# A hybrid layer on one core: the attention heads' tiles keep their places, and ScalarE's work within a step is put in another order

## The reference

```
z      = q k^T / sqrt(128)                     for all keys up to the query
log_1m = log_sigmoid(-z)     (0 where masked)
later  = sum of log_1m over the keys between this key and the query
w      = exp(log_sigmoid(z) + later)           (0 where masked)
out    = w v,   then out * silu(g)
```

## Time and profile before

| | |
|---|---|
| median of three executions | 2375.96 us |
| the profiled execution: time, span | 2375.72 us, 2373.8 us |
| PE busy | 2320.7 us, 98% of the span |
| DVE busy | 1498.2 us, 63% |
| POOL busy | 1262.6 us, 53% |
| ACT busy | 1060.0 us, 45% |
| granted clock of PE | 0.997 of full |

### The profile page before, as it was taken

One profiled execution on the slowest core, in us unless ns is written; L12 is line 12 of the kernel. 1 busy time (PEld: TensorE's weight loads), 2 busy tenths in 40 slices (PEclk: granted clock), 3 DMA queues, 4 the chain that ended last, 5 costly groups with the idle time before them and its releaser, 6 DMA issues. The chain is left out here.

```text
span 2373.8 us, 30066 instructions
## 1 busy us (share of the span) xinstructions
PE 2320.7 (98%) x10928; PEld 1907.3 (80%) x10928; DVE 1498.2 (63%) x1682; ACT 1060.0 (45%) x1659; POOL 1262.6 (53%) x819
## 2 busy tenths in 40 slices
PE   8999999999999999999999999999999999999998
PEld 5788878888877888888788887788888777888887
DVE  6566742664496465458788888733754586466366
ACT  4455542343375255332465666632342583255220
POOL 1566643874366355435476675744864555445331
PEclk9999999999999999999999999999999999999999
DMA  5544332123213312373444444322133123412442
GB/s 203 186 155 151 125 107 93 54 80 124 94 58 119 130 49 74 101 290 118 124 134 133 149 143 136 125 76 85 49 108 132 60 59 112 142 60 76 132 178 80
DMA packets 99186, 273.19 MB, mean 115 GB/s; under 512 B 9312, under 2 KB 30944, under 8 KB 98016
## 3 DMA queue, kind: packets, MB, share of 16 engines
q1 hardware_dynamic: 97600, 266.56, 34.1%
q10 hardware_dynamic: 1440, 4.72, 0.6%
HBM read 208.33 MB, written 62.91 MB: 114 GB/s over the span
## 5 line engine op out<-in xcount | busy, mean ns | idle before, releaser
L2147 POOL TENSOR_TENSOR WLS<-SR,WHS 128x512 fp32r<-128x512 f32 x264 | 422.4, 1619 | 172.5 <-ACT WHS L1043 165.4
L720 PE MATMUL J<-XBH,WHS 128*128 128x512 f32 x1152 | 454.3, 394 | 4.9 <-ACT ST L1114 4.2
L722 PE MATMUL J<-XBH,WLS 128*128 128x512 f32 x1152 | 449.7, 390 | 0.0
L721 PE MATMUL J<-XBL,WHS 128*128 128x512 f32 x1152 | 449.4, 390 | 0.0
L720 PE MATMUL J<-XBH,WH 128*128 128x512 f32 x864 | 342.7, 397 | 2.5 <-DVE XBL L1564 1.7
L722 PE MATMUL J<-XBH,WL 128*128 128x512 f32 x864 | 337.5, 391 | 0.0
L721 PE MATMUL J<-XBL,WH 128*128 128x512 f32 x864 | 337.1, 390 | 0.0
L2190 POOL TENSOR_TENSOR REST<-REST,SHARE 128x512 f32<-128x512 f32 (+3 forms) x160 | 205.1, 1290 | 115.3 <-DVE REST L1752 109.9
L720 PEld LDWEIGHTS J<-XBH,WHS 128*128 128x128 f32 x1152 | 216.8, 188 | 52.3 <-ACT ST L1114 5.9
L2139 POOL TENSOR_TENSOR SR<-RAW 128x512 f32<-128x512 f32 x71 | 117.0, 1648 | 265.7 <-DMA RAW<-w 233.6
L1597 DVE TENSOR_TENSOR ST<-J,ST 128x512 f32<-128x512 f32 x160 | 109.5, 685 | 232.8 <-PE J L722 191.9
(11 more groups left out here) (331 smaller groups left out, 4836.4 us busy)
## 6 DMA issues: line engine op xcount, KB each, us to landing
RAW<-w SPq DMA_DIRECT2D x144, 512.0 KB, 3.7
pk_m<-MB SPq DMA_DIRECT2D x56, 512.0 KB, 5.0
MB<-pk_m SPq DMA_DIRECT2D x48, 512.0 KB, 4.1
KC<-pk_k SPq DMA_DIRECT2D x40, 512.0 KB, 5.9
VC<-pk_v SPq DMA_DIRECT2D x40, 512.0 KB, 4.6
BRAW<-w SPq DMA_DIRECT2D x64, 256.0 KB, 5.1
XRAW<-xt SPq DMA_DIRECT2D x8, 1024.0 KB, 12.5
pk_v<-STL SPq DMA_DIRECT2D x16, 512.0 KB, 4.8
```

Source lines behind the costliest of these rows:

```text
L720: nc.tensor.matmul(to, wh, xh, start=first, stop=True, skip_group_check=True)
L721: nc.tensor.matmul(to, wh, xl, start=False, stop=True, skip_group_check=True)
L722: return nc.tensor.matmul(to, wl, xh, start=False, stop=True, skip_group_check=True)
L2147: low = G_.tensor_tensor(WLS[:, k, :], SR[:, k, :], WHS[:, k, :].bitcast(F32), ALU.subtract)
```

## The change

- **Places.** Within a half the queries, keys and values of all heads stay in the same three tiles (`places`). So the first copy of a head's first pair (queries) waits for the product with the last gate (`sil`) and no longer for the stored values; the second copy (keys) waits for the stored low part of the values; the stored high part is waited for only by the next pair's first copy. `v_kept` is two semaphores, and the low part is stored first.
- **ACT's order in a step.** `KEEP` of step `s`, then the high part of step `s - 4`, then the pieces, then `SHARE` of step `s`.
- **Fill.** `LEAD` is 2 pieces for the last three heads of the second half. At every fourth step the half pieces come before the product with the values on PE, and the shares change.
- **Loads.** The first head's two key blocks are loaded after piece 9 instead of 12 of the pair before it.
- **POOL.** For the pairs within the heads the fourth sum of weight tiles moves from piece 11 to piece 12.

```diff
-LEAD = 4
+LEAD = ((4, 4, 4, 4), (4, 2, 2, 2))
...
-    return 1 if with_values(s) else 6 if half and s >= NS[half] else 4 if half else 2
+    return 1 + (s % BLOCKS == 0) if with_values(s) else 6 if half and s >= NS[half] else 4 if half else 2
...
+        def places(half, of):
+
+            return of[half], of[half + 1], of[(half + 2) % 3]
...
-                o = g // PAIRS * HEADS + i // 2
-                if i % 2:
-                    return ST[(o + 2) % 3][:, ::-1], ST[o % 3][:]
-                return ST[o % 3][:], ST[(o + 1) % 3][:, ::-1]
+                q, k, v = places(g // PAIRS, ST)
+                return (v[:, ::-1], q[:]) if i % 2 else (q[:], k[:, ::-1])
...
-                for part, of in enumerate((STL[(hh + 2) % 3], STL[(hh + 1) % 3])):
+                for part, of in ((1, places(half, STL)[1]), (0, places(half, STL)[2])):
                     sp.wait_ge(v_blk, 2 * hh + 2)
...
-                pair(g0 + 1, {2: last_rows, 12: first_keys})
+                pair(g0 + 1, {2: last_rows, 9: first_keys})
...
                     if s < ns:
                         scores(half, h, s)
-                    if with_values(s) and s < ns + TAIL:
-                        values(half, h, 2 * ((s - TAIL - 2) // BLOCKS) + (s % BLOCKS == 0))
+                    first = with_values(s) and s < ns + TAIL and s % BLOCKS != 0
+                    if first:
+                        values(half, h, 2 * ((s - TAIL - 2) // BLOCKS))
                     for k in range(halves_filled(half, h, s - 1), halves_filled(half, h, s)):
                         piece(*fill[k // 2], (k % 2,))
+                    if with_values(s) and s < ns + TAIL and not first:
+                        values(half, h, 2 * ((s - TAIL - 2) // BLOCKS) + 1)
...
-                    if i % 2 == 0:
-                        wait_if(act, v_kept, 32 * hh)
-                    elif p:
+                    if i % 2 == 0 and p:
+                        wait_if(act, v_kept[1], 16 * hh)
+                    elif i % 2 == 0 and i:
+                        act.wait_ge(sil, half * NB * KB + i // 2)
+                    elif i % 2 and p:
                         act.wait_ge(q_kept, 16 * (hh + 1))
-                    elif i > 1:
-                        act.wait_ge(sil, half * NB * KB + i // 2)
+                    elif i % 2:
+                        wait_if(act, v_kept[0], 16 * hh)
...
                 for s in range(ns + TAIL + 1):
+                    if s < ns:
+                        keeps(half, h, s)
                     if 0 <= s - TURN - 1 < ns:
                         turned_hi(half, h, s - TURN - 1)
-                    if s < ns:
-                        shares(half, h, s)
                     if s == ns and h + 1 < HEADS:
                         load_queries(half, h + 1)
                     if s:
                         for g, i in fill[filled(half, h, s - 2):filled(half, h, s - 1)]:
                             piece(g, i)
+                    if s < ns:
+                        shares(half, h, s)
...
-                elif i == 11:
-                    if apart:
-                        rest_of_sums(g + 1, False, (1,))
+                elif i == 11 and apart:
+                    rest_of_sums(g + 1, False, (1,))
+                elif i == (12 if apart else 11):
                     sum_raw(g + 1, 3)
```

More of the change, by code:

```diff
@@ L142, in halves_filled @@
     part = sum(share_of(half, t) for t in range(min(s + 1, NS[half] + TAIL)))
-    made = 2 * LEAD + (n - 2 * LEAD) * part // whole
+    made = 2 * LEAD[half][h] + (n - 2 * LEAD[half][h]) * part // whole
     return made if half else made // 2 * 2
@@ L433, in keep_keys @@
                 hh = half * HEADS + h
-                for part, of in enumerate((KHT[h % 2], STL[(hh + 1) % 3])):
+                for part, of in enumerate((KHT[h % 2], places(half, STL)[1])):
                     sp.wait_ge(k_lo, hh + 1)
@@ L458, in load_v @@
                 if i == 0:
-                    sp.wait_ge(v_kept, 32 * (half * HEADS + h + 1))
+                    for kept in v_kept:
+                        sp.wait_ge(kept, 16 * (half * HEADS + h + 1))
                 wait_if(sp, pv_done, 2 * n)
@@ L780, in turn @@
                 hh = g // PAIRS * HEADS + g % PAIRS // 2
[L781 removed]
+                v, c = places(g // PAIRS, ST)[2], J[(g + 1) % 2]
                 if part:
@@ L1074, in room @@
                     if i == 0:
[L1075 to L1078, removed]
+                        if half and not p:
+                            act.wait_ge(q_kept, 16 * HEADS * (half + 1))
+                            act.wait_ge(sil, half * NB * KB + HEADS)
+                        elif half or not p:
+                            act.wait_ge(k_kept, 32 * HEADS * (half + 1))
+                            act.wait_ge(v_kept[1], 16 * HEADS * (half + 1))
+                        else:
+                            act.wait_ge(v_kept[0], 16 * HEADS * (half + 1))
                     elif p:
                         act.wait_ge(w_done, S_END[half])
+                    elif half:
+                        act.wait_ge(v_kept[0], 16 * HEADS * (half + 1))
+                    else:
+                        act.wait_ge(q_kept, 16 * HEADS * (half + 1))
+                        act.wait_ge(sil, half * NB * KB + HEADS)
                 elif kind == "merge":
@@ L1146, in values_hi @@
                 act.wait_ge(v_tr, 2 * hh + part + 1)
-                nc.scalar.copy(STL[(hh + 2) % 3][:, part * C:(part + 1) * C], J[(g + 1) % 2][:]).then_inc(v_hi, 1)
+                nc.scalar.copy(places(g // PAIRS, STL)[2][:, part * C:(part + 1) * C], J[(g + 1) % 2][:]).then_inc(v_hi, 1)
             def split_keys(g):
@@ L1156, in split_keys @@
                     act.wait_ge(o_ready, TB * half)
-                nc.scalar.copy(KHT[h % 2][:], ST[(half * HEADS + h + 1) % 3][:]).then_inc(k_hi, 1)
+                nc.scalar.copy(KHT[h % 2][:], places(half, ST)[1][:]).then_inc(k_hi, 1)
             def pair(g, after={}):
@@ L1214, in _, with keeps @@
             unit_hi(0, 5)
-            def shares(half, h, s):
+            def keeps(half, h, s):
                 gs = first_step(half, h) + s
@@ L1227, in shares @@
                                      ).then_inc(rest_done, 1)
+            def shares(half, h, s):
+                gs = first_step(half, h) + s
+                n = C - STEPS[half][s][3]
                 wait_if(act, w_done, gs - 1)
@@ L1262, in attention @@
                 act.wait_ge(k_kept, 32 * (half * HEADS + h + 1))
-                silu_of(half, 0, h, half * PAIRS + 2 * h + 1, ST[(half * HEADS + h) % 3][:])
+                silu_of(half, 0, h, half * PAIRS + 2 * h + 1, places(half, ST)[0][:])
                 for g, i in fill[:filled(half, h, -1)]:
@@ L1782, in attention @@
                     output(half, h - 1, 1)
-                silu(half, 0, h, ST[(half * HEADS + h) % 3][:])
+                silu(half, 0, h, places(half, ST)[0][:])
                 for g, i in fill[:filled(half, h, -1)]:
```

12 lines of the change are left out of this document (7 added, 5 removed).

## The result

The changed kernel takes 2379.18 us, the median of 22 executions, against 2375.86 us for 22 of the kernel before: a ratio of 1.0014, 95% interval 1.0007 to 1.002. It is slower by 0.14%, where 17 us less were forecast. The profiled execution took 2377.70 us, with a span of 2375.9 us against 2373.8.

A forecast was written before the change was run, and what follows sets the result against it. PE, busy for 98% of the span, was taken as the bound, with its idle and half-clock time to win. Terms -4.95 - 6.46 - 2.7 - 4.8 - 2.7 + 3.0 + 1.6 = -17.0 us gave 2358.7 us, range 2348 to 2371.

The forecast's parts named there:

- the diagonal blocks: Cast behind `KEEP`, which waits for DVE's mask: up to 1 us a step, reaching PE in the last heads; +3.0 us.
- The starts: First head of each half: earlier key blocks, low part stored first; -4.95 and -6.46 us, 12.4 less with the copies.
- The two other waits for copies in the first half: First half: two more PE waits for copies, which stood for `v_kept`, go; 1.0 us of the -2.7.
- the clock's part: At both starts PE no longer idles, so half-clock stretches go: 1.70 us in the first half, 3.0 in the second.
- Half pieces ahead of the values, the last heads, the second `LEAD`: Waits filled: second half's first three heads -4.8 us; first half's last head 1.7; second half's last head, `LEAD` 2, -2.7.
- `SHARE` behind the pieces: On ACT, the pieces' casts and copies delay `SHARE` by 0.6 to 1.6 us; four waits of 0.41, +1.6 us.
- The slower rival: `SHARE` becomes late at 36 steps with a wide cast, 0.7 us each: 25 us more, 2389 us; chance 0.08.
- POOL's sum at nothing: POOL's fourth sum moves one piece later at no cost: next weights 2 pieces from use, POOL busy 64.2 of 91.2 us.
- the bound of DVE and POOL: Rival: DVE and POOL bound the heads, PE's fills return as later waits; 10.8 us won, 2365 us; chance 0.17.
- The port rule: DVE and POOL exclude each other on shared SBUF ports, so an earlier DVE scan may cost POOL 0.72 us each.

The follow-up runs named there:

- the starts alone: Changed kernel with ScalarE's order, fill and POOL's sum as in the kernel before; places, split waits and early key blocks kept: 2365.64 us, ratio 0.9961.
- the new fill and the sum back: Changed kernel with ScalarE's old order (cast, `KEEP`, `SHARE`, pieces) and POOL's fourth sum back at piece 11: 2365.03 us, ratio 0.9959.

## Why the prediction was wrong, step by step

- **The step that failed is the one on the diagonal blocks, in how far it reaches.** Its mechanism came: DVE has nothing to split until the mask, `KEEP` and the cast are done, "up to 1 us a step, four steps a head"; measured are 0.92 us at each of 32 blocks. But the step let that reach PE only in the last heads, where turns already waited for DVE: +3.0, with 8 as the upper end. The cast's place alone costs 17.5 us on the kernel before and 15.8 on the changed one, outside the bounds; in the two middle heads of the second half, for which the prediction had nothing, 3.3 and 3.1 us arise from the diagonal on (changed kernel against the one with the cast first). DVE was busy there for 77.5 of 91.2 us, but idle time elsewhere in the head did not take up a delay in each step of the diagonal. The step also left out whole blocks, where the cast comes late as well (median 1.23 us); there DVE's idle time differs by 0.9 us with the cast alone moved on the changed kernel, and by 9.8 on the kernel before.
- The same change turned a second sentence round. The prediction said of the values' waits that they could fall by more than the 0.70 us "because DVE's work itself begins sooner", since the cast left a split and a `SHARE` behind. It did leave those, and got `KEEP` in front instead, with the scores or the mask that `KEEP` waits for.
- **The starts: right within what can be told.** -12.4 with the copies; measured -9.1 by the medians, where the interval reaches from 5.9 to 12.3, and -11.5 by the profiled spans. Two terms in it do not show. The two other waits for copies in the first half (-1.0) did not go with `v_kept`: with the starts alone there are three of 0.5 us, and only `SHARE` behind the pieces took them away. And the clock's part (1.70 + 3.0) finds no support: of the 46 executions of the kernel before in the experiments, five with a mean clock of 0.999 took 2375.45 us on average and nine with 0.997 took 2375.76, where 0.002 of the span would be 4.75 us. Nor does a wait alone bring the clock down: it stayed at 1.00 behind the changed kernel's 3.0 us for `VC` (to 1216.4), and fell to 0.50 for 3.4 us (from 1214.5) behind the 2.9 us for `VC` with the cast first.
- **Half pieces ahead of the values, the last heads, the second `LEAD`: right in place, wrong in worth.** With ScalarE's old order the waits ahead of the values fell from 15.3 to 8.6 us, 6.7 of the 9.2 forecast (1.7 + 4.8 + 2.7). But the time is that of the starts alone (2365.76 and 2365.64): waits of ACT's copies rose from 1.8 to 4.4 us, `VC` from 0.8 to 2.3, and PE's transposes of `ST` (L791) from 1.8 to 3.7. The run with the old fill and the late sum has copies and transposes at 1.1 and 1.8 us, so these two come with the fill. Its waits for `VC` are 3.3, and the run with the new fill and the sum back has 0.7, so those come with the sum in these kernels. The 0.68 of these terms stands in no row; with the 0.70 of the earlier trace rows they would be 0.2 us larger.
- **`SHARE` behind the pieces:** +1.6 forecast; 0 to -2.4 measured from kernel to kernel, within what the runs can tell apart. The slower rival built on it fell too: waits for `SHARE` are 1.0 us. So a loss came, but by none of the mechanisms that the rivals priced.
- **POOL's sum at nothing:** right in the sum, though not for the reason given: a weight load on SP waits for it and `VC` stands behind that load, but POOL's product takes back what `VC` loses.
- The range's upper end was also added up too low: the bound of DVE and POOL with the diagonal and `SHARE` at twice their prices is 2375.7 - 12.4 + 6.0 + 3.2 = 2372.5, not 2371. The measured 2379.18 lies beyond both.
- Put in the place of the forecast's terms, the differences from kernel to kernel are -9.1 (the starts), 0.1 (fill and sum), -2.2 (`SHARE`) and +15.6 (the cast), together +4.4 against +3.3 measured; the rest is the 1.1 us by which the kernel before differs between these groups of runs. Each kernel differs from the next by one of these steps, so the sum has to come out; it shows where the time went and does not test it.
- Another page of the Trainium skill, "Perfetto Trace Analysis", section "Identifying Performance Opportunities", says to optimize the most contended engine first, and takes the busy share as the measure for VectorE, ScalarE and GpSimd. Here 15 us hung on the order of ScalarE's work, whose share is the lowest of the four computing engines (45% before, 44% after).
- The port rule that was weighed did not decide: the 96 full scans took 1813 ns on average before and 1763 after. But the rows agree with it more fully than the prediction read them. The product of POOL beside the scan of 2.00 us in the earlier trace rows began before it:

```profile
1481.41 1.28 POOL L2190 TENSOR_TENSOR REST<-REST,SHARE 128x512 f32<-128x512 f32 x1 [1.89 <-DVE REST L1752]
```

It ends at 1482.69, and the scan 1.07 us later. So the scan's 2.00 us hold the rest of the product and then the scan's own work; they are shorter than both on end because the product was under way. Of the 82 such scans of the kernel before that took over 1.4 us, 81 began while POOL was at an instruction, and 76 of them ended 1.0 to 1.15 us after it.

## What to carry to other kernels

When two instructions of an in-order engine change places, ask for each what it waits for: the one that now stands behind can't begin before the inputs of the one in front are there. So a short instruction with early inputs that another engine waits for should not go behind one that waits for a slower engine, however idle its own engine is; least of all behind one that waits for the very engine it serves. Here DVE's mask released `KEEP`, `KEEP` stood ahead of the cast, and DVE waited for the cast. Price such a swap at every step of the loop, and don't take the idle share of a whole head as room in one step. The Trainium skill's page "PSUM — Partial Sum Buffer", section "Engine vs sequencer instructions", says that ScalarE's queue is strictly first in, first out. The trace agrees: with `KEEP` in front, the cast began 1.23 us (median) after its transposes were done, and 0.04 us with the old order.

## What the runs showed that was not expected

A late cast is paid where DVE has nothing else to do meanwhile. `KEEP`'s waits for PE's scores rose by 44.5 us over the span, and DVE's idle time ahead of the low parts at whole blocks by 5.9; the round from the mask over `KEEP` and the cast back to DVE cost it 0.92 us at each block of the diagonal, and 13 of PE's 17 waits ahead of the product follow a DVE that was not idle just then, but late. And work put over waits need not shorten the time: the new fill covered 6.7 us of them, and 6.0 came up elsewhere.
